# Loading the modulation matrix's chunks from GpSimd's queue instead of SyncE's

## The reference

```
cond = silu(c)
for l in range(2):
    mod = (cond @ mod_w[l] + mod_b[l]).reshape(B, 9, D)       # mod_w[l] is 1024 x 9216
    h = modulate(rmsnorm(x, norm_g[l, 0]), mod[0], mod[1])    # h * (1 + scale) + shift
    x = x + 0.5 * mod[2] * swiglu(h, ffn_w1[l, 0], ffn_w2[l, 0])
    h = modulate(rmsnorm(x, norm_g[l, 1]), mod[3], mod[4])
    x = x + mod[5] * mixer(h)
    h = modulate(rmsnorm(x, norm_g[l, 2]), mod[6], mod[7])
    x = x + 0.5 * mod[8] * swiglu(h, ffn_w1[l, 1], ffn_w2[l, 1])
return rmsnorm(x, final_norm_g)
```

## Time and profile before

| what | value |
|---|---|
| median of 3 runs | 2339.55 us (2336.26 to 2340.13) |
| profiled execution: time, span of its instructions | 2333.04 us, 2331.2 us |
| PE busy | 2188.9 us, 94% |
| PE weight loads busy | 2077.2 us, 89% |
| DVE busy | 1518.2 us, 65% |
| ACT busy | 1154.8 us, 50% |
| POOL busy | 35.9 us, 2% |
| HBM read | 423.86 MB, 182 GB/s over the span |
| `mod_raw` loads | 144 of 512 KB from SP, 5.2 us median from issue to landing |

### The profile page before, as it was taken

One profiled execution on the slowest core, in us unless ns is written; L12 is line 12 of the kernel. 1 busy time (PEld: TensorE's weight loads), 2 busy tenths in 40 slices (PEclk: granted clock), 3 DMA queues, 4 the chain that ended last, 5 costly groups with the idle time before them and its releaser, 6 DMA issues.

```text
span 2331.2 us, 43089 instructions
## 1 busy us (share of the span) xinstructions
PE 2188.9 (94%) x16944; PEld 2077.2 (89%) x16944; DVE 1518.2 (65%) x2582; ACT 1154.8 (50%) x1852; POOL 35.9 (2%) x38
## 2 busy tenths in 40 slices
PE   9989978999999997899889999899899999999998
PEld 8989957999999995899879999699899998658998
DVE  7766386775776648677467656677655555785554
ACT  5434565543553456554355445655345444454543
POOL 0002000000000200000000000000000000000000
PEclk9999989999999998999989999899999999699999
DMA  7865412775677541277548654257655454203544
GB/s 274 302 237 186 176 55 85 273 263 190 221 274 237 189 164 51 100 271 261 184 167 275 241 178 149 81 205 271 197 175 183 165 196 146 73 1 119 185 167 142
DMA packets 78053, 426.09 MB, mean 183 GB/s; under 512 B 9696, under 2 KB 10464, under 8 KB 47632
## 3 DMA queue, kind: packets, MB, share of 16 engines
q1 hardware_dynamic: 77968, 424.95, 53.2%
HBM read 423.86 MB, written 1.05 MB: 182 GB/s over the span
## 4 chain that ended last, share of the span: by engine, by line
PE 81%; DVE 11%; ACT 4%; issue 2%; DMA 1%; DVEq 0%; ACTq 0%
PE bank L390 24%; PE bank L391 24%; PE bank L392 24%; DVE slot_lo L1117 3%; DVE h L1167 2%; DMA mod_raw<-in_mod_w_dram 1%; ACT slot_hi L805 1%; ACT L811 1%; PE bank L717 1%; PE bank L418 1%; DVE room L1390 1%; PE bank L420 1%; PE bank L419 1%; PE bank L519 1%; DVE room L1402 1%
## 5 line engine op out<-in xcount | busy, mean ns | idle before, releaser
L390 PE MATMUL bank<-h_hi,slot_hi 128*128 128x256 f32 x3552 | 1015.1, 286 | 30.9 <-DVE slot_lo L1117 11.5
L1117 DVE TENSOR_TENSOR slot_lo<-slot,slot_hi 128x1024 fp32r<-128x1024 f32 (+1 forms) x728 | 791.0, 1108 | 363.1 <-ACT slot_hi L805 359.7
L391 PE MATMUL bank<-h_lo,slot_hi 128*128 128x256 f32 x3552 | 1007.5, 284 | 0.0
L392 PE MATMUL bank<-h_hi,slot_lo 128*128 128x256 f32 x3552 | 1007.2, 284 | 0.0
L805 ACT ACTIVATE slot_hi<-slot 128x1024 fp32r<-128x1024 f32 (+1 forms) x728 | 660.1, 957 | 316.8 <-PE bank L392 303.7
L390 PEld LDWEIGHTS bank<-h_hi,slot_hi 128*128 128x128 f32 x3552 | 684.1, 193 | 42.2 <-issue 29.5
L391 PEld LDWEIGHTS bank<-h_lo,slot_hi 128*128 128x128 f32 x3552 | 684.4, 193 | 1.8 <-issue 1.7
L392 PEld LDWEIGHTS bank<-h_hi,slot_lo 128*128 128x128 f32 x3552 | 684.2, 193 | 0.0
L390 PE MATMUL bank<-act_hi,slot_hi 128*128 128x256 f32 x1408 | 402.8, 286 | 34.0 <-DVE slot_lo L1117 34.0
L391 PE MATMUL bank<-act_lo,slot_hi 128*128 128x256 f32 x1408 | 401.5, 285 | 0.0
L392 PE MATMUL bank<-act_hi,slot_lo 128*128 128x256 f32 x1408 | 401.1, 285 | 0.0
(11 more groups left out here) (222 smaller groups left out, 1678.5 us busy)
## 6 DMA issues: line engine op xcount, KB each, us to landing
slot<-in_slots_dram SPq DMA_DIRECT2D x236, 1024.0 KB, 5.0
slot<-in_wd_dram SPq DMA_DIRECT2D x128, 704.0 KB, 4.1
mod_raw<-in_mod_w_dram SPq DMA_DIRECT2D x144, 512.0 KB, 5.2
room<-in_na_bias_dram SPq DMA_DIRECT2D x8, 512.0 KB, 5.0
x<-in_x_dram SPq DMA_DIRECT2D x1, 1024.0 KB, 5.1
out_dram<-h SPq DMA_DIRECT2D x4, 256.0 KB, 2.4
cond<-in_cond_dram SPq DMA_DIRECT2D x1, 512.0 KB, 9.4
lru_w<-in_lru_w_dram SPq DMA_DIRECT2D x1, 512.0 KB, 6.1
```

The lines of the kernel that those rows point to most:

```text
L390: pe.matmul(o, slot_hi[b][:, w:w + P], x_hi, start=first, stop=False, skip_group_check=skip)
L391: pe.matmul(o, slot_hi[b][:, w:w + P], x_lo, start=False, stop=False, skip_group_check=skip)
L392: return pe.matmul(o, slot_lo[b][:, w:w + P], x_hi, start=False, stop=last, skip_group_check=skip)
L1117: ins = dve.tensor_tensor(slot_lo[b][:, c0:c1], slot[b][:, c0:c1], slot_hi[b][:, c0:c1].bitcast(F32), ALU.subtract)
```

## The change

`load_mod` leaves SP's stream, and the same 144 loads are issued from POOL's stream by a new `load_mods` (L356 of the changed kernel). Buffers, sizes, the semaphore that each load raises and the wait before it (`mod_read` at least c - 1) are the same. Since POOL has work of its own, the loads are cut in four runs around it: chunks 0 to 25 before the first mixer's bias, 26 to 73 before the second's, 74 to 121 before the two products of the second block's first mixer, and 122 to 143 at the end.

```diff
--- before.py
+++ after.py
@@ -285,14 +285,6 @@
                     load_slot(n)
                 return first + count
 
-            def load_mod(c):
-
-                if c >= MOD_CHUNKS:
-                    return
-                if c >= 2:
-                    sp.wait_ge(s["mod_read"], c - 1)
-                sp.dma_start(mod_raw[c % 2][:, :], a["mod_w"][c, :, :]).then_inc(s[MOD_READY[c % 2]], 16)
-
             def load_constants(*which):
                 for dst, name in which:
                     sp.dma_start(dst, a[name]).then_inc(s["const_ready"], 16)
@@ -307,8 +299,6 @@
             sp.dma_start(gains[:, :, :], a["gains"]).then_inc(s["gains_loaded"], 16)
             n = load_slots(0, RING)
             sp.dma_start(cond[:, :], a["cond"]).then_inc(s["cond_loaded"], 16)
-            load_mod(0)
-            load_mod(1)
             constants_after = {
                 4: ((mod_b[:, :], "mod_b"), (ident[:, :], "ident"), (na_mask[:, :, :], "na_mask"),
                     (na_gain[:, :, :], "na_gain"), (gla_gain[:, :], "gla_gain"), (w_gate[:, :, :], "w_gate"),
@@ -327,15 +317,11 @@
                     n += 1
                     if ffn == 0 and c == 2:
                         sp.dma_start(wide_mask, a["gla_mask"]).then_inc(s["mask_loaded"], 16)
-                    if c >= 4 and ffn < MOD_GROUPS:
-                        load_mod(ffn * MOD_GROUP + c - 2)
                     if ffn == 0 and c in constants_after:
                         load_constants(*constants_after[c])
                 for j in range(KC):
                     for half in range(2):
                         load_down_slot((ffn * KC + j) * 2 + half)
-                        if j < 3 and ffn < MOD_GROUPS:
-                            load_mod(ffn * MOD_GROUP + FC - 2 + 2 * j + half)
                     if bias is not None and j % 2 == 1:
                         load_bias(bias, j // 2)
                 return n
@@ -362,8 +348,17 @@
         def _(pool):
             seen = Seen()
 
+            def load_mods(first, past):
+
+                for c in range(first, min(past, MOD_CHUNKS)):
+                    if c >= 2:
+                        pool.wait_ge(s["mod_read"], c - 1)
+                    pool.dma_start(mod_raw[c % 2][:, :], a["mod_w"][c, :, :]).then_inc(s[MOD_READY[c % 2]], 16)
+
+            load_mods(0, 2)
             for layer in range(LAYERS):
 
+                load_mods(2 * layer * MOD_GROUP + 2, (2 * layer + 1) * MOD_GROUP + 2)
                 pool.wait_ge(s["const_ready"], 16 * CONST_LOADS)
                 pool.wait_ge(s["bias_ready"], seen("bias_ready", 16 * BIAS_PARTS))
                 for head in range(NA_HEADS):
@@ -371,6 +366,8 @@
                         v = na_bias[:, head, qt * S:qt * S + S]
                         pool.tensor_tensor(v, v, na_mask[:, :, :].rearrange("p a b -> p (a b)"),
                                            ALU.add).then_inc(s["bias_masked"], 1)
+                load_mods((2 * layer + 1) * MOD_GROUP + 2, (2 * layer + 2) * MOD_GROUP + 2)
+            load_mods(2 * LAYERS * MOD_GROUP + 2, (2 * LAYERS + 1) * MOD_GROUP + 2)
 
             flat = lambda v: v[:, :, :].rearrange("p a b -> p (a b)")
             pool.wait_ge(s["lru_gate_ready"], seen("lru_gate_ready", 4))
@@ -379,6 +376,7 @@
             pool.wait_ge(s["gelu_ready"], seen("gelu_ready"))
             pool.tensor_tensor(mix[:, 0:4, :].rearrange("p a b -> p (a b)"), flat(xc),
                                proj[:, 8:10, :].rearrange("p a b -> p (a b)"), ALU.mult).then_inc(s["mix_raw"], 1)
+            load_mods((2 * LAYERS + 1) * MOD_GROUP + 2, MOD_CHUNKS)
 
 
         @block.tensor
```

## The result

The changed kernel takes 2342.31 us in the median of 20 runs (2338.62 to 2351.59), the kernel before 2336.62 us in 20 runs made beside them. The ratio is 1.0025, with a 95% interval of 1.0013 to 1.0037: slower by 5.8 us (3.0 to 8.7). The forecast's 2342.3 is met to the microsecond, but partly by luck. It was +2.7 us on a median of three runs that was 2.9 us higher than that of the 20. The loss is twice what I summed, and the likeliest case, "within 0.2%", is just missed.

A forecast was written before the change was run, and what follows sets the result against it. PE was taken as the bound, with 81% of the chain. Terms 0 + 1.0 + 0.6 + 1.1 + 0 = 2.7 us on 2339.55 gave 2342.3 us, range 2336 to 2351.

The forecast's parts named there:

- within 0.2%: Whole kernel: time within about 0.2%, 4.7 us, of no change; chance 0.50.
- The six waits: DVE's waits for chunk 23 ending the hidden stage of FFNs 0 to 5: 0 added, bounds 0 and 7.0 us.
- E: Extra time a POOL load needs from end of wait to first byte, against SP: 0.67 us, bounds 0 to 2.19.
- The slow-issue rival: POOL issues late in the six waits: with E = 2.19, 9.7 us slower, 2349.3 us; chance 0.30.
- DVE keeps POOL from building the load: At chunk 23, POOL cannot work beside DVE's read of chunk 22: E 2.18 us, 9.7 us slower; chance 0.08.
- landing differs by over 1 us: Sign of being wrong: chunk 23's landing was to stay at 4.5 to 6.3 us after issue.
- The bias ahead of chunk 23: FFNs 0 and 2: SP's bias load, now ahead of chunk 23, delays it 0.5 us each, 1.0 in two.
- Chunk 24 behind chunk 23: Next group's chunk 24, sent 1.5 us behind chunk 23 on one queue, costs 0.1 us each, 0.6 in all.
- The start: Chunks 0 and 1 load beside x, delaying ACT's first square: 1.1 us, between 0 and 2.3.
- Steady steps and POOL's own work: Hidden steps' slots sharing with chunks, and POOL's masks behind its loads: 0 added; steady steps' bound 4.8 us.
- The faster rival: Separate queue lands chunk 23 in 3.7 us: six links 9.0 us shorter, 2331.7 us in all; chance 0.10.
- the lower clock: After longer waits PE may run at a lower granted clock: some 2 us in six, only for the high end.

The follow-up runs named there:

- the edit: The changed kernel with the next group's chunks 24 and 25 held on POOL until the down stage's first residual: 2334.7 us in one run, later 2343.7 us, ratio 1.0022.
- both_undone: The changed kernel with the first bias load of FFNs 0 and 2 and the next group's chunks 24 and 25 held back: 2344.3 us, ratio 1.0025.
- the delays: Tiny ACT operations ahead of the first square: four or nine on the kernel before, ratio 0.9997 each; nine on the changed kernel, 1.0029.

## Why the prediction was right or wrong

- **The six waits: 0, right.** In the four FFNs without a bias they went from 13.6 to 13.8 us, the mean of four profiles each. E comes out near what I took. POOL's issue starts 0.3 us after DVE's read of chunk 21 ends (SP's in before 0.03), and in the four FFNs without a bias the first bytes follow after 1.23 to 1.41 us, against SP's 0.77: E is 0.7 to 0.9 us (0.67 taken), under the 1.02 us of cover. The slow-issue rival needed 1.35. FFN 4 in after:

```profile
1326.49 0.53 POOL L356 DMA_DIRECT2D mod_raw<-in_mod_w_dram  x1 [5.24 <-DVE mod_raw L1183]
1328.04 0.53 POOL L356 DMA_DIRECT2D mod_raw<-in_mod_w_dram  x1 [1.01 <-DVE mod_raw L1183]
```

```profile
1324.97 1.22 DVE L1183 SCALAR_TENSOR_TENSOR mod_raw<-mod_raw,cond 128x1024 f32<-128x1024 f32 x1
...
1326.51 1.23 DVE L1183 SCALAR_TENSOR_TENSOR mod_raw<-mod_raw,cond 128x1024 f32<-128x1024 f32 x1
1327.66 0.08 DVE L1183 DVE_READ_ACCUMULATOR mod_raw<-mod_raw,cond 128x1 f32 x1
1330.92 1.23 DVE L1183 SCALAR_TENSOR_TENSOR mod_raw<-mod_raw,cond 128x1024 f32<-128x1024 f32 x1 [3.18 <-DMA mod_raw<-in_mod_w_dram]
```

  POOL issues chunk 23 at 1326.49, while DVE works on chunk 22 from 1326.51 to 1327.74, and the chunk lands at 1330.89. POOL's instruction runs beside DVE's, and the first bytes come 1.34 us after it starts, where the rival "DVE keeps POOL from building the load" needed 2.7. So that rival falls. By my own sign "landing differs by over 1 us" I would be wrong in FFNs 3 and 5 (6.00 and 6.23 became 4.87 and 4.93), but a second profile of before has 4.99 and 4.82 there: it is the profile that I started from that was off.
- **The bias ahead of chunk 23: 1.0, measured 1.6** (10.62 less 8.98, the mean of 8.93 and 9.03; one pair of profiles, 5.17 + 5.49 against 4.44 + 4.49, gives 1.7). Against before, where this bias part went out behind chunk 23, the two links grew by 1.3 us (9.3 to 10.6, means of four). The place was right. The mechanism was not sharing to the end, as I had it, but a start 1.5 us later.
- **Chunk 24 behind chunk 23: 0.6, measured 0.8** in six, on two profiles of the edit and within the spread of the others. Together the two terms were 1.6 and measure 2.4; the waits grew by 2.1 us between the means of four profiles each, 1.9 of it in FFNs 0 and 2.
- **The start: 1.1, measured 0.** I said that the first square would move to 6.9 us. It is where the earlier trace rows has it:

```profile
1.25 1.20 POOL L356 DMA_DIRECT2D mod_raw<-in_mod_w_dram  x2 [0.81 <-POOLq L1825]
...
5.79 1.15 ACT L818 ACTIVATE sq<-x 128x512 f32<-128x512 f32 x2 [3.29 <-DMA x<-in_x_dram]
```

  POOL's first load is issued at 1.25 us, but its first bytes come at 5.08, when x is nearly in. It was the case "POOL starts late", which I gave half the weight.
- **Steady steps and POOL's own work: 0, right,** but one sentence was not: I said that no wait of ACT for a slot would appear, and one did, in FFN 4's down stage:

```profile
1341.40 1.48 ACT L803 ACTIVATE slot_hi<-slot 128x704 fp32r<-128x704 f32 x2 [5.81 <-DMA slot<-in_wd_dram]
```

  In before ACT stood 4.71 us at this place for PE, so the slot is about 1.1 us late. PE has work left from the slots ahead and waits for nothing there.
- **The faster rival fell.** Its 3.7 us of the first byte plus bytes, and the estimated 3.2 us by the Trainium skill's fit (DMA: Bandwidth & Descriptors, Anatomy of one DMA), face landings of 4.4 to 5.5 us here. The slot ahead still has the engines, as in the earlier trace rows.
- **The step that failed: the lower clock.** I named it only for the range's high end, "some 2 us in six", tied to longer waits. The runs have 10.5 us more at the lower level, 5.2 us of time, with the waits put back too. Over all these runs the span grew by 5.3 us, so it is as good as the whole loss. My two terms of transfer order are there at equal clock on one chip (2.2 us by `both_undone`), but the time does not follow them. Why loads from another queue make PE's clock lower stays open. It does not go away with the longer waits (`both_undone`), nor with a shift of 2 us (the delays). That leaves the rhythm inside the steps, or POOL's own activity; I tried neither alone. Loading only the first two chunks, or only the rest, from POOL was not tried either.

## What to carry to other kernels

Before moving a load to another queue, ask what releases it: if it goes out at the moment its buffer is free, the queue cannot help, and moving the read that waits for it can (here 1.5%, with the loads left where they were). When a small difference is in question, take span times granted clock of many runs beside the time; it tells a cost of the work from a cost of the clock, to a microsecond or two. And do not build on a single profile: its links differed by 1.7 us among like stages, where a second one of the same kernel had all six within 0.9. The same goes for a window of the clock: compare windows that start at the same point of the work, in several profiles of each kernel.

## What the hardware showed that was not expected

- A load of 512 KB from POOL keeps it busy for 0.53 us. At the four hidden ends without a bias, behind a 704 KB slot, its first bytes come 1.2 to 1.4 us after it starts; SP's slot had its own after 0.77. In the hidden steps of after, where a 1 MB slot was the last thing SP sent, they come after 2.25 us in the median.
- POOL's first load of the program had its first bytes 3.8 us after its issue; the two first chunks landed after 10.0 us in the median.
- With a down slot and a bias part standing on SP's queue, POOL's load got its first bytes only after 2.75 to 2.85 us, in all six profiles with that order.
- Beside sixteen POOL additions of 128x256 that ran back to back, two DVE operations took 12.41 us, which take 1.69 us in FFN 4. It is seen once; elsewhere the same sixteen took 14.5 to 15.4 us.
- Moving only DMA issues, with every matmul the same, lowered PE's mean granted clock from 0.964 to 0.962 (116 and 78 runs).
